# Two gated feed-forward layers: each pair of tiles of the first matrix as seven block products, the second matrix in four passes between them

## What is computed

```python
def conv_ffn(h, g_norm, w_in, conv_w, conv_b, w_out):
    L = h.shape[1]
    xn = rms_norm_2(h, g_norm)
    a, b = jnp.split(xn @ w_in, 2, axis=-1)          # 1024 -> 2 x 2816
    ap = jnp.pad(a, ((0, 0), (CONV_W - 1, 0), (0, 0)))
    a_conv = conv_b
    for j in range(CONV_W):                          # width 3
        a_conv = a_conv + ap[:, j:j + L] * conv_w[j]
    return h + (jax.nn.silu(a_conv) * b) @ w_out     # 2816 -> 1024
```

## Time and profile before

| | |
|---|---|
| median of 3 runs | 3136.31 us (3134.22 to 3138.06) |
| the profiled execution | span 3134.2 us |
| PE busy | 2990.2 us, 95% |
| DVE, ACT, POOL busy | 65%, 40%, 37% |
| first matrix, layer 0 / layer 1 | 249.62 / 241.09 us of the chain |
| second matrix, layer 0 / layer 1 | 128.47 / 122.85 us of the chain |

### The profile page before, as it was taken

One profiled execution on the slowest core, in us unless ns is written; L12 is line 12 of the kernel. 1 busy time (PEld: TensorE's weight loads), 2 busy tenths in 40 slices (PEclk: granted clock), 3 DMA queues, 4 the chain that ended last, 5 costly groups with the idle time before them and its releaser, 6 DMA issues.

```text
span 3134.2 us, 47541 instructions
## 1 busy us (share of the span) xinstructions
PE 2990.2 (95%) x17673; PEld 2612.4 (83%) x17673; DVE 2025.2 (65%) x3238; ACT 1261.6 (40%) x2075; POOL 1157.7 (37%) x564
## 2 busy tenths in 40 slices
PE   6999999998999999999999999899999998999998
PEld 3766679998988888888887788699999975799986
DVE  4767515999977778788886255466651375466622
ACT  3347333446963333333333334432222446432221
POOL 2420333664014444455553222044444430244442
PEclk9998999999999999999999999799999999999999
DMA  6710223555679999999996211023223420122231
GB/s 247 280 60 1 62 93 96 166 175 191 227 248 350 346 328 341 337 351 350 346 347 229 75 55 41 14 88 94 87 88 101 117 81 1 41 89 93 94 101 67
DMA packets 179876, 509.22 MB, mean 162 GB/s; under 512 B 14881, under 2 KB 72353, under 8 KB 175393
## 3 DMA queue, kind: packets, MB, share of 16 engines
q1 hardware_dynamic: 72288, 262.57, 25.4%
q0 software_dynamic: 37440, 136.40, 11.9%
q10 hardware_dynamic: 70016, 108.54, 10.3%
HBM read 467.60 MB, written 39.85 MB: 162 GB/s over the span
## 4 chain that ended last, share of the span: by engine, by line
PE 87%; ACT 5%; DVE 4%; issue 2%; DMA 1%; ACTq 0%; DVEq 0%
PE ps L1279 23%; PE ps L1230 17%; PE ps L1167 16%; PE ps L1533 8%; PE ps L901 8%; ACT arena L1960 2%; PE ps L1351 2%; PE ps L952 1%; ACT arena L1976 1%; PE ps L1680 1%; PE ps L1299 1%; PE ps L1457 1%; PE ps L1414 1%; PE ps L654 1%; PE ps L1421 1%
## 5 line engine op out<-in xcount | busy, mean ns | idle before, releaser
L2314 POOL TENSOR_TENSOR w_lo<-ring,w_hi 128x1024 fp32r<-128x1024 f32 x300 | 755.0, 2520 | 1387.9 <-ACT w_hi L795 1387.8
L795 ACT ACTIVATE w_hi<-ring 128x1024 fp32r<-128x1024 f32 x500 | 525.4, 1055 | 771.9 <-PE ps L1230 277.4
L1230 PE MATMUL ps<-w_hi,arena_r 128*128 128x512 f32 x1536 | 426.8, 397 | 4.5 <-DVE arena_r L2772 4.5
L1167 PE MATMUL ps<-h_hi,w_hi 128*128 128x384 f32 x1024 | 355.5, 347 | 5.0 <-issue 5.0
L1230 PEld LDWEIGHTS ps<-w_hi,arena_r 128*128 128x128 f32 x1536 | 289.0, 189 | 72.2 <-DVE arena_r L2772 5.0
L1167 PE MATMUL ps<-h_lo,w_hi 128*128 128x384 f32 x1024 | 348.9, 341 | 0.0
L1279 PE MATMUL ps<-h_hi,w_hi 128*128 128x264 f32 (+2 forms) x1536 | 347.5, 298 | 0.6 <-DVE arena L2869 0.5
L1167 PE MATMUL ps<-h_hi,w_lo 128*128 128x384 f32 x1024 | 346.4, 338 | 0.0
L1279 PE MATMUL ps<-h_lo,w_hi 128*128 128x264 f32 (+2 forms) x1536 | 346.2, 297 | 0.0
L1279 PE MATMUL ps<-h_hi,w_lo 128*128 128x264 f32 (+2 forms) x1536 | 345.6, 297 | 0.0
L2327 POOL DMA_INDIRECT arena<-u_rows,arena x128 | 193.4, 1511 | 375.8 <-DVE arena L2748 354.5
(11 more groups left out here) (343 smaller groups left out, 5444.0 us busy)
## 6 DMA issues: line engine op xcount, KB each, us to landing
ring<-weight_stream SPq DMA_DIRECT2D x500, 512.0 KB, 3.7
gates<-arena ACTq DMA_DIRECT2D x12, 2048.0 KB, 7.3
arena<-gates ACTq DMA_DIRECT2D x32, 768.0 KB, 14.3
arena<-w_modulation ACTq DMA_DIRECT2D x17, 1024.0 KB, 5.3
early_acts<-arena ACTq DMA_DIRECT2D x64, 192.0 KB, 2.7
arena<-early_acts ACTq DMA_DIRECT2D x32, 384.0 KB, 7.7
arena<-w_modulation ACTq DMA_DIRECT2D x2, 2560.0 KB, 15.0
x<-x_t ACTq DMA_DIRECT2D x1, 2112.0 KB, 19.5
```

Of the source, the lines that this page charges most:

```text
L795: act.activation(w_hi[:, s, :], ring[:, s, :], ACT.Copy).then_inc(hi_ready, 1)
L1167: last = pe.matmul(ps[:, bank, 0:ND], w, v, start=c == 0 and p == 0, stop=c == DC - 1 and p == 2)
L1230: last = pe.matmul(ps[:, Y_BANKS[b][half], :], a[u], w[v][:, half * BANK:(half + 1) * BANK], start=first and p == 0, stop=final and p == 2)
L2314: pool.tensor_tensor(w_lo[:, s, :], ring[:, s, :], w_hi[:, s, :], ALU.subtract)\
```

## The change

**The first matrix.** For a pair, the outputs (tile a, tile b) x (first half of the tokens, second half) and the input features (even chunks, odd chunks) are seen as 2x2 blocks. Their product is made of seven block products of 4 chunks x 3 matmuls x one half of the tokens (12 matmuls), not eight. The seven take sums of the blocks: `S1` to `S4` of the weights (`weight_sum`, on DVE, four 128x512 operations for each pair, straight from the ring) and three sums of the tokens (`ffn_t1`, `ffn_w`, made once a layer in `out_add`, with their own high and low parts `t_hi`, `t_lo`). Weights go through `w_hi` and `w_lo` by halves of 512 columns, eight halves deep (HALVES): one half is one unit of PE's list (`FFN_UNITS`). A pair's units are A11, A22 of the pair before, S1, A12, S2, S4, S3. Three units (S2, S3, A22) go on top of A11's sum in the same bank, S4 on top of S1's, and ACT copies the sum out in between (`keep_product`, four 128x264 copies a pair). DVE adds the pieces (`join_a` twice, `join_b`), and multiplies by `r_tok` (`norm_a`). The first tap moves from DVE to ACT (`first_tap`). In layer 1 both tiles now have two halves of 258 tokens.

**The second matrix.** It is made in four passes over 6, 6, 6 and 4 pairs: the first three stand behind pair 6, 12 and 18, each 12 units of four 128x128 blocks (24 matmuls of 264 columns, or 12 of 512), the last (8 units) at the end. Each pass adds all eight output tiles to `x` (`add_out`). 18 of its 22 slots come not through the ring but from a second tensor, `ffn_out`, into one buffer in the first two passes and two in the third (`out_raw`, `out_buffer`, `load_out`), still on SP's queue.

All loops of the two layers are written out. The other lines of the diff count semaphores anew (`ahead`, `used`) and let several of them serve twice; they change no work.

```diff
+FFN_PARTS = (6, 6, 6, 4)
+FFN_FIRST = (0, 6, 12, 18)
+HALVES = 2 * RING
+PASS_UNITS = 12
+def ffn_units():
+    units, out = [], 0
+    for f in range(FC):
+        units += [("A11", f)] + ([("A22", f - 1)] if f else []) + [("S1", f), ("A12", f), ("S2", f)]
+        units += [("S4", f), ("S3", f)]
+        if f in FFN_FIRST[1:]:
+            for _ in range(PASS_UNITS):
+                units.append(("out", out))
+                out += 1
...
+            def load_out(k, q):
...
+                    before = q - 1 if q <= PASS_UNITS else q - 2
+                    sp.wait_ge(lo_ready, unit0(k) + UNIT["out", 2 * before + 1] + 1)
+                sp.dma_start(out_raw[k][out_buffer(q)], ffn_out_d[k * TAIL_SLOT + q])\
+                    .then_inc(out_in[out_buffer(q)], 16)
...
+                def product(m, bank, src, ready, start, stop):
+                    w = half_of(w_hi, m), half_of(w_lo, m)
+                    for j in range(DC // 2):
+                        ready(j)
+                        for p, (u, v) in enumerate(three(src(j), (w[0][:, j * P:(j + 1) * P], w[1][:, j * P:(j + 1) * P]))):
+                            last = pe.matmul(ps[:, bank, 0:width], u, v, start=start and j == 0 and p == 0,
...
+                    pe.wait_ge(lo_ready, U0 + m + 1)
+                    if kind == "A11":
+                        wait(pe, ffn_gated, 2 * F0 + 2 * f - 2)
...
+                    elif kind == "S1":
+                        wait(pe, a_joined, 2 * F0 + 2 * f)
...
+                    elif kind == "S4":
+                        pe.wait_ge(p_kept, C0 + 4 * f + 2)
...
+                for m, (kind, f) in enumerate(FFN_UNITS):
+                    act.wait_ge(slot_used, U0 + m + 1)
+                    if kind in KEPT:
+                        keep_product(kind, f)
...
+                    if m + HALVES < NUNITS:
+                        half_high(k, m + HALVES)
...
+                    if kind == "S3":
+                        first_tap(f)
+                    elif kind == "A22":
+                        silu(f)
+                    elif kind == "A12" and f:
+                        high_gated(f - 1)
...
+            def half_lows(k):
+                for m in range(NUNITS):
+                    pool.wait_ge(hi_ready, unit0(k) + m + 1)
+                    pool.tensor_tensor(half_of(w_lo, m), raw_half(k, m), half_of(w_hi, m), ALU.subtract).then_inc(lo_ready, 1)
...
+                if kind == "S1":
+                    last = dve.tensor_tensor(dst[0], b[:, 0:BANK], b[:, BANK:], ALU.add)
+                elif kind == "S2":
+                    dve.wait_ge(s_added, S0 + 1)
+                    last = dve.scalar_tensor_tensor(dst[1], dst[0], -1.0, a[:, 0:BANK], ALU.mult, ALU.subtract)
...
+                for f in range(FC):
+                    if f:
+                        gate(f - 1)
+                    if f + 1 < FC:
+                        weight_sum(k, "S4", f + 1)
+                        weight_sum(k, "S3", f + 1)
+                    join_a(f, 0)
+                    if f:
+                        low_gated(f - 1)
...
+                    join_a(f, 1)
+                    norm_a(f)
+                    if f + 2 < FC and f not in FFN_FIRST[1:]:
+                        weight_sum(k, "S1", f + 2)
+                        weight_sum(k, "S2", f + 2)
+                    taps(f)
+                    join_b(f)
```

More of the change, by code:

```diff
@@ L86 @@
 TURNS = _t
+FFN_PARTS = (6, 6, 6, 4)
+FFN_FIRST = (0, 6, 12, 18)
+LIVE = 12
+HALVES = 2 * RING
+PASS_UNITS = 12
+PRODUCTS = ("A11", "A22", "S1", "A12", "S2", "S4", "S3")
+SUMS = ("S1", "S2", "S4", "S3")
+KEPT = ("A11", "S1", "S2", "S3")
+def ffn_units():
[7 more added lines that the diff above has]
+                out += 1
+    units.append(("A22", FC - 1))
+    for o in range(out, DC * FC // 4):
+        units.append(("out", o))
+    return units
+FFN_UNITS = ffn_units()
+NUNITS = len(FFN_UNITS)
+UNIT = {u: m for m, u in enumerate(FFN_UNITS)}
+OUT_SLOTS = DC * FC // 8
+TAIL_SLOT = 3 * PASS_UNITS // 2
+RING_SLOTS = 2 * FC + OUT_SLOTS - TAIL_SLOT
+ADDS = len(FFN_PARTS) * DC
+LATER = NUNITS - RING_SLOTS
 VEC = {}
@@ new lines, in out_unit, with outs_within, out_banks, out_tokens @@
+        def out_unit(p, t):
+            n = FFN_PARTS[p]
+            return UNIT["out", p * PASS_UNITS + (t * n + n - 1) // 4]
+        def outs_within(first, end):
+            return [(p, t) for p in range(len(FFN_PARTS)) for t in range(DC) if first <= out_unit(p, t) < end]
+        def out_banks(k, p, t):
+            return ps[:, 2 * (t % 2), 0:L - META] if k else ps[:, 2 * (t % 2):2 * (t % 2) + 2, 0:HALF]
+        def out_tokens(k, a):
+            return a[:, META:L] if k else a.rearrange("p (a b) -> p a b", a=2)
@@ L827, in used @@
         def used(turn, s):
-            return turn * RING + (s + 1)
+            return turn * RING + (s + 1 + ahead(turn))
         V_SLOT, ROPE_SLOT, Q_SLOT = 10, 8, 12
@@ L880, in _, with load_turns @@
                 sp.dma_start(ring[:, s, :], stream[s]).then_inc(slot_loaded[s], 16)
[L881 to L885, removed]
+            def load_turns(first, end):
+                with sp.Fori(first, end) as i:
+                    for s in range(RING):
+                        sp.wait_ge(lo_ready, i * RING + (s + 1 - RING + ahead(first)))
+                        sp.dma_start(ring[:, s, :], stream[bass.ds(i * RING + s, 1), :, :]
+                                     .rearrange("o p n -> (o p) n")).then_inc(slot_loaded[s], 16)
@@ L1519, in ffn @@
[L1519 to L1535 removed]
+                halves = FFN_HALVES[k]
```

587 lines of the change are left out of this document (419 added, 168 removed).

## The result

The changed kernel takes 3320.02 us (median of 4 runs, 3318.02 to 3323.47) where the kernel before takes 3136.16 (3134.22 to 3138.06): a ratio of 1.059, 95% interval 1.0575 to 1.0605. The forecast was 3248 with 3115 to 3310. The direction held, and so did the main mechanism, the turns; the size did not: 183.9 us slower where 111.8 were forecast, 10 us above the top of the range.

The account below looks back on a forecast made before the run. PE, busy 95% of 3134.2 us, bounded the kernel; DVE, in turns with POOL, would then set the pairs. Layer 0 +43.6, layer 1 +48.0, starts and ends +20: total +111.6, about 3248 us, range 3115 to 3310.

Parts of the forecast that it names:

- The products removed: First matrix on PE: 84 matmuls a pair for 96, 10.28 and 10.08 us a pair, together 60.1 us less PE work.
- Turns between DVE and POOL: DVE operations reading two SBUF buffers and POOL subtractions take whole turns: 2.26 us per 1024 columns on POOL, 0.57 on DVE.
- the products set the pace: Rival: DVE and POOL do not exclude each other, both stay under PE's 10.28 us a pair; 3091 us; chance 0.14.
- depth absorbs the turns: Rival: DVE wins the turns, POOL lives on its eight halves ahead; 3154 us, or 3131 without buffer cost; chance 0.14.
- The pair: First matrix: DVE, taking turns with POOL, sets each pair at 14.0 us in layer 0 and 13.8 in layer 1.
- The last pass: End of a layer: PE runs out of work before pair 21 is ready, 7 us (2 to 10).
- The start of a layer: Token sums hang on the last output tile, some 5.5 us against 4.4 on PE; 3 us with the norm's chain (0 to 6).
- The buffer: Single slot buffer in the first two passes: loads come late, 5.8 us for each pass, 11.6 us a layer.
- What the passes give back: DVE and POOL catch up in passes; DVE may then lag 4.4 us until S1 waits for `join_a`: 17.6 us off a layer.
- The clock: Rival: PE's stalls lower its clock; at 1.2 GHz a pair's matmuls take 20.6 us, both layers +286, 3534 us; chance 0.04.
- the longest pair: Case where POOL never runs in DVE's other 3.2 us: 16.7 and 16.4 us a pair, about 3365 us in all.
- the starts and ends of the layers: Token sums at each layer's start and the wait for pair 21 at its end: 10 us a layer, +20 together.

## Why the prediction was right in kind and wrong in size

**The products removed.** Right: 84 matmuls take 10.25 us when nothing holds them up, forecast 10.28.

**Turns between DVE and POOL.** Right as a mechanism: without POOL's subtraction DVE's operations fall to 0.69 us; with the subtractions moved to DVE, more work takes less time; with one input in PSUM the same operation loses its wait. That a third of PE's work can go and the pair stays excludes PE as what sets it. These runs alone would also fit ports that the two engines divide; that the turns are whole is shown by the timeline, where DVE's operations end 0.54 to 0.57 us behind the end of a subtraction. The Trainium skill's rule ("SBUF — State Buffer", SBUF: two separate sides), that the shared ports are locked and not divided, agrees with the timeline. The rivals that the products set the pace, or that depth absorbs the turns, are out: no stretch of the changed kernel ran at PE's pace.

**The pair was mis-sized: this is the step that failed most.** The prediction took "14.0, near the lower end" between 13.5 and 16.7; measured are 14.8 and 14.7 against 14.0 and 13.8. DVE's own work is 7.8 us a pair (its busy time without turns), not the 8.8 that the prediction had with the wait for the Silu; so strictly one after the other would be 7.8 + 7.9 = 15.7, and 13.5 with POOL running in all of DVE's room. The measured 14.8 lies between, nearer the upper end: seven turns cost DVE's cycle 7.0 us, 1.0 each. "POOL mostly has work waiting" was the wrong support: in the second stretch POOL sits idle 26 us of 91 for ACT's high parts, and ACT, by the same view, 14.7 us for the taps ahead of the Silu, with POOL's next halves behind it in its list. So POOL does not always have a subtraction at hand when DVE leaves it room; how much of the 1.3 us between 13.5 and 14.8 that explains was not measured, and stays open. 22 x 0.8 + 22 x 0.9 is 37.4 of the 72.1 us missed.

**The last pass.** The forecast was 7 us over PE's work (2 to 10). Layer 0 has 42.9 us for 192 matmuls of 0.122 us, 23.4, so 19.5 over it; layer 1 has 30.6 for 22.3, so 8.3. The wait for pair 21 was foreseen (5.1 us in the trace of either layer). Not foreseen was layer 0's loop through ACT's scaled parts, which makes PE wait 5.5 and 2.7 us, and that PE's work itself takes longer at a lower granted clock: 29.6 us busy for 23.4, at 0.80 in this window, and 25.4 for 22.3 in layer 1, at 0.89. Together the two layers are 13.8 us over the forecast.

**The start of a layer.** Forecast 3 us; the output tiles take 53.1 and 53.7 us where the same matmuls took 47.3 and 47.0, so 5.8 and 6.7 us more, because the four weight sums stand ahead of a tile's addition. That is 6.5 us above the forecast in all. Moving the sums shortened the stage and lengthened the first stretch, so the term belonged to DVE's and POOL's arrears and was not one of its own. The first stretch has some 3.6 us a layer besides: 108.9 us in layer 0, less 6.1 for the buffer, where seven pairs of 14.8 less 4.4 are 99.2.

**The buffer.** Right: 5.8 us forecast; 6.1 and 6.4 measured in layer 0 and 5.5 and 6.4 in layer 1, in the stretches ahead of passes 1 and 2 as said. In the second stretch ACT is idle for a DMA 10.4 us.

**What the passes give back.** Right in size: the third stretch has six pairs in 84.4 us, which is 6 x 14.8 less the 4.4 of the working. But the prediction took the 4.4 from a wait before S1, for `join_a`. Of the gaps that it foresaw, before S1 and before S4 and S3, the long one stands before S4, for ACT's copy, and none before S1 in the second and third stretch. So that the number came out is in part luck.

**The clock.** In layer 0's stretches it was 0.87 to 0.96, not at the 1.2 GHz level throughout, and by the run with fewer matmuls it cost nothing in the pairs: there 0.78 goes with a pair no longer. The first three passes of layer 0 are back at 0.97 to 1.00. The rows agree with the Trainium skill's warning of stalls between bursts ("TensorE: Matmul & The Clock Gate", HAM oscillation); the lower clock is seen to cost time in the last passes, where the work hangs on PE.

These terms make 37.4 + 13.8 + 6.5 + 1.2 (buffer) + 7.2 (first stretches) = 66 of the 72 us; the remaining 6 were not followed. The range failed at its upper end. The prediction's own sum with the longest pair (16.7 and 16.4 us) gave 3365, and the range stopped at 3310; the measured pair alone stays inside it (3248 + 37 = 3285), and the starts and ends of the layers, to which the prediction gave 20 us in all, carried the time over.

## What to carry to other kernels

When two engines share a resource in whole turns, add both engines' times for it to one queue before counting what a third engine saves: here some 1.4 us of matmuls a pair were bought with seven more of DVE's operations that take turns (eleven for four) and seven short subtractions of POOL for two long ones, and until then all turns had been hidden behind PE. The best repair found that keeps the whole computation was to give the slower engine's work to the faster, though that was the busier one. Here an operation with an input in PSUM paid no turn (0.42 us for 128x264, 0.69 for 128x516), so it matters which operations read what. And where a change ends a layer's reserve of finished work, follow one tile around the loop of engines at the end, rather than adding their durations: in each engine's list, look for work of another stage that stands ahead of the tile.

## What was not expected of the hardware

A DVE queue with 123 operations was busy 69.57 us where one with 82 was busy 81.81, in the same stretch. POOL's 512-column subtraction takes from 1.26 us up to 1.81, on DVE it takes 0.685; so taking turns hurts the slower engine's work as well. And a turn relieved at one operation comes back at another: with two operations freed, the taps grew by 0.47 us each (two a pair), yet the pair as a whole gained 1.0 us; two turns of 0.57 us would be 1.1.
